# Sample value pages in TensorE: one page at a time with VectorE taking six of sixteen, against four pages at a time in four column strips

## What is computed

```python
def diff_attn(q, k, v, q_pos, k_pos, lam):
    s = jnp.einsum('bqhcd,bkhcd->bhcqk', q, k).astype(jnp.float32) * (DK ** -0.5)
    ...
    p = jax.nn.softmax(s, axis=-1)
    a = p[:, :, 0] - lam * p[:, :, 1]
    return jnp.einsum('bhqk,bkhd->bqhd', a.astype(v.dtype), v)

def mem_attn(q, mk, mv):
    ...
    return jnp.einsum('bhqm,bmhd->bqhd', p.astype(mv.dtype), mv)

k_past = cache_k[l][page_table].reshape(DB, -1, N_HEADS, 2, DK)
v_past = cache_v[l][page_table].reshape(DB, -1, N_HEADS, DV)
```

## Time and profile before

| what | value |
|---|---|
| median of 3 runs | 3238.03 us (3236.7 to 3238.45) |
| profiled execution, first to last instruction | 3223.0 us |
| around the span, up to the median | 15.0 us |
| the profiled execution's own time, taken as the median | 3238.0 us |
| TensorE busy (matmuls) | 2664.7 us, 83% |
| VectorE busy | 1416.9 us, 44% |
| GpSimd busy | 956.0 us, 30% |
| ScalarE busy | 351.2 us, 11% |
| moved by DMA | 921.73 MB, 286 GB/s |

### The profile page before, as it was taken

How to read it: one execution, slowest core, us unless ns; L and a number is a source line. 1 busy time by engine, 2 the same in 40 slices (tenths; PEclk the granted TensorE clock), 3 DMA queues, 4 the chain that set the end, 5 groups by cost and what they waited for, 6 DMA issues and landing times.

```text
span 3223.0 us, 31001 instructions
## 1 busy us (share of the span) xinstructions
PE 2664.7 (83%) x9169; PEld 1617.1 (50%) x9169; DVE 1416.9 (44%) x2212; ACT 351.2 (11%) x796; POOL 956.0 (30%) x961
## 2 busy tenths in 40 slices
PE   6899999785899999999999367776677777777778
PEld 5687888673433358888877222222222322222232
DVE  1456569533233321200026865555644444444431
ACT  3111000124200000000021000001000000011010
POOL 1256661100122210000000354444444444444432
PEclk9899999896899999999999789999999999999999
DMA  5599996740588763544434499999899999999997
GB/s 165 193 316 333 323 351 223 256 147 0 183 270 270 268 197 127 161 156 130 130 105 130 180 402 392 397 378 374 362 422 421 422 421 421 422 422 422 422 422 303
DMA packets 306118, 921.73 MB, mean 286 GB/s; under 512 B 15738, under 2 KB 196050, under 8 KB 236244
## 3 DMA queue, kind: packets, MB, share of 16 engines
q0 software_dynamic: 123488, 731.93, 57.2%
q1 hardware_dynamic: 182548, 188.92, 18.1%
HBM read 914.19 MB, written 6.63 MB: 286 GB/s over the span
## 4 chain that ended last, share of the span: by engine, by line
PE 56%; DMA 31%; DVE 6%; issue 4%; ACT 1%; POOL 1%; POOLq 0%; ACTq 0%; DVEq 0%; SPq 0%
DMA sb_hT<-in_peer_v_dram,sb_ring 26%; PE ps L531 19%; PE ps L608 10%; PE ps L814 7%; PE ps L618 5%; PE ps L719 5%; PE ps L598 3%; DMA sb_wring<-in_peer_u_dram,sb_ring 2%; DVE sb_S L1605 1%; PE ps L835 1%; POOL sb_wring L450 1%; PE ps L728 1%; PE ps L687 1%; DMA sb_bregion<-in_w_conv_out_dram 1%; PE ps L517 1%
## 5 line engine op out<-in xcount | busy, mean ns | idle before, releaser
L1605 DVE CUSTOM_DVE_ANT_0 sb_S<-sb_wring,sb_rows 128x2048 f32<-128x2048 f32 x256 | 586.9, 2292 | 542.2 <-DMA sb_wring<-in_peer_u_dram,sb_ring 531.9
L814 PE MATMUL ps<-sb_bregion,sb_ring 128*128 128x512 f32 x1024 | 490.0, 625 | 245.9 <-DMA sb_bregion<-in_peer_v_dram,sb_ring 243.8
L814 PE MATMUL ps<-sb_hT,sb_ring 128*128 128x512 f32 x1024 | 472.3, 605 | 160.9 <-DMA sb_hT<-in_peer_v_dram,sb_ring 159.9
L531 PE MATMUL ps<-sb_hT,sb_wring 128*128 128x264 f32 x2304 | 528.9, 391 | 4.6 <-ACTq L906 2.0
L531 PEld LDWEIGHTS ps<-sb_hT,sb_wring 128*128 128x128 f32 x2304 | 440.1, 192 | 85.3 <-issue 9.0
L814 PEld LDWEIGHTS ps<-sb_bregion,sb_ring 128*128 128x128 f32 x1024 | 192.7, 197 | 542.2 <-issue 241.7
L814 PEld LDWEIGHTS ps<-sb_hT,sb_ring 128*128 128x128 f32 x1024 | 185.6, 191 | 447.4 <-issue 266.0
L608 PE MATMUL ps<-sb_hT,sb_wring 128*128 128x264 f32 x1536 | 372.6, 394 | 20.6 <-DMA sb_bregion<-in_w_conv_out_dram 20.6
L450 POOL DMA_INDIRECT sb_wring<-in_peer_u_dram,sb_ring x264 | 319.8, 1211 | 214.2 <-DVEq L1062 84.9
L608 PEld LDWEIGHTS ps<-sb_hT,sb_wring 128*128 128x128 f32 x1536 | 286.5, 191 | 122.9 <-issue 77.4
L450 POOL DMA_INDIRECT sb_bregion<-in_peer_v_dram,sb_ring x132 | 154.3, 1169 | 253.2 <-PE ps L814 222.0
(11 more groups left out here) (327 smaller groups left out, 1949.6 us busy)
## 6 DMA issues: line engine op xcount, KB each, us to landing
sb_wring<-in_w_in_dram SPq DMA_DIRECT2D x52, 2048.0 KB, 11.5
sb_rows<-in_cache_v_dram POOLq DMA_DIRECT2D x128, 512.0 KB, 4.8
sb_ring<-in_cache_k_dram POOLq DMA_DIRECT2D x64, 512.0 KB, 6.3
sb_mkv<-in_cache_k_dram POOLq DMA_DIRECT2D x64, 512.0 KB, 6.3
sb_wring<-in_w_mem_kv_dram SPq DMA_DIRECT2D x8, 2048.0 KB, 9.1
sb_wring<-in_w_o_dram SPq DMA_DIRECT2D x8, 2048.0 KB, 8.0
sb_wring<-in_w_peer_q_dram SPq DMA_DIRECT2D x8, 2048.0 KB, 8.3
sb_ring<-in_cache_mem_k_dram POOLq DMA_DIRECT2D x16, 512.0 KB, 6.9
```

Of the source, the lines that this page charges most:

```text
L531: last = mm(ps[:, (2 * r + c) % 4, 0:NT], wring[:, r, k, c * P:(c + 1) * P], rhs[:, k, :], start=(k == 0), stop=(k == KC - 1))
L814: last = mm(ps[:, bank + q, :], diag[:, j % 4, :], e_slots[j % 4][:, q * 512:(q + 1) * 512], start=False, stop=False, skip_group_check=True)
L1605: st(V.tensor_tensor_reduce(out=work, in0=u_slots[slot], in1=h2, scale=1.0, scalar=0.0, op0=ALU.mult, op1=ALU.add, accum_out=out))
```

## The change

TensorE takes all 16 pages. `values` is called after steps 2, 7, 12, 17 and 22 of a chunk and takes four blocks at a time (the last time two). Block n uses the 32 columns of the array, and the 32 partitions of PSUM, that begin at 32 x (n modulo 4). Its weights are 32 columns of `zst` from its own first on, so the columns after its own heads belong to other pages. Blocks of the same strip add up in PSUM. It waits for all blocks of the group first, then goes over them once for each half of the page, so that four neighbouring matmuls lie in four strips. Each block's second matmul gives its buffer back. One ring has six buffers, in the space of the two rings before, and GpSimd issues the 18 loads of a token in order. `mask_sums` works on 64 (memory) and 128 (pages) partitions instead of 4 and 8, with `head_rows`, a 128 x 8 pattern that is 1 where a partition's number modulo 32 is the head's; three small additions make it once. It waits for the pages by `vpage_used`. `columns` of the memory blocks comes after step 8 instead of 5. VectorE's weighing is gone.

```diff
-        VR, DR = 4, 2
+        VR = 6
-        DP = 6
-        PV = 2 + PAGES - DP
-        weighed = work[:, 0:DC]
-        own_heads = [sq_mkv[0:n, o:o + DC] for n, o in ((MH, 2 * DC), (HEADS, 3 * DC))]
+        VB = 2 + PAGES
+        QUAD = 32
+        own_heads = [sq_mkv[0:n, o:o + DC] for n, o in ((2 * QUAD, 2 * DC), (P, 3 * DC))]
+        head_rows = stat[:, 48:48 + HEADS]
...
             with pool.Fori(0, TS) as b:
-                for k in range(DP):
-                    for n in (2 * k, 2 * k + 1, PV + k):
-                        if n < PV:
-                            pool.wait_ge(s["vpage_used"], b * PV + (n + 1))
-                            r = n % VR
-                        else:
-                            pool.wait_ge(s["dpage_used"], b * DP + (k + 1))
-                            r = VR + k % DR
-                        ...
-                        pool.dma_start(v_slots[r], src).then_inc(v_landed[r], 16)
+                for n in range(VB):
+                    pool.wait_ge(s["vpage_used"], b * VB + (n + 1))
+                    ...
+                    pool.dma_start(v_slots[n % VR], src).then_inc(v_landed[n % VR], 16)
...
-            def values(i, k, n):
-                if n < PV:
-                    pe.wait_ge(v_landed[n % VR], i * (4 * (PV // VR) * 16) + 16 * (PV // VR * k + n // VR + 1))
-                    block = v_slots[n % VR]
-                else:
-                    pe.wait_ge(s["weighed_ready"], i * 4 + (k + 1))
-                    block = weighed
-                ...
-                for q in range(2):
-                    last = mm(ps[0:w.shape[1], bank + q, :], w, block[:, q * 512:(q + 1) * 512], start=first, stop=final)
-                last.then_inc(s["vpage_used" if n < PV else "weighed_used"], 1)
+            def values(i, k, n0):
+                if n0 == 0:
+                    pe.wait_ge(s["sums_masked"], i * 8 + (2 * k + 1))
+                blocks = range(n0, min(n0 + 4, VB))
+                for n in blocks:
+                    pe.wait_ge(v_landed[n % VR], i * (4 * (VB // VR) * 16) + 16 * (VB // VR * k + n // VR + 1))
+                for q in range(2):
+                    for n in blocks:
+                        g = n % 4
+                        if n < 2:
+                            bank, w0, first, final = 6, PAGES * HEADS + n * MH, True, True
+                        else:
+                            bank, w0, first, final = 4, (n - 2) * HEADS, n < 6, n >= VB - 4
+                        last = mm(ps[g * QUAD:(g + 1) * QUAD, bank + q, :], zst[:, k % 2, w0:w0 + QUAD],
+                                  v_slots[n % VR][:, q * 512:(q + 1) * 512], start=first, stop=final)
+                        if q == 1:
+                            last.then_inc(s["vpage_used"], 1)
...
-                            if step % 5 in (0, 2, 4) and todo:
-                                values(i, k, todo.pop(0))
-                            if step == 5:
+                            if step % 5 == 2:
+                                values(i, k, 4 * (step // 5))
+                            if step == 8:
                                 columns(i, k, 0)
...
+            st(TT(head_rows[:, :], ident[:, 0:HEADS], ident[:, QUAD:QUAD + HEADS], ALU.add))
+            st(TT(head_rows[:, :], head_rows[:, :], ident[:, 2 * QUAD:2 * QUAD + HEADS], ALU.add))
+            st(TT(head_rows[:, :], head_rows[:, :], ident[:, 3 * QUAD:3 * QUAD + HEADS], ALU.add))
...
-                n = (MH, HEADS)[kind]
-                if kind == 0:
-                    dve.wait_ge(s["vpage_used"], i * (4 * PV) + (PV * k + 2 + VR))
-                else:
-                    dve.wait_ge(s["weighed_used"], i * 4 + (k + 1))
+                n, heads = own_heads[kind].shape[0], (MH, HEADS)[kind]
+                dve.wait_ge(s["vpage_used"], i * (4 * VB) + (VB * k + (2, VB)[kind] + VR))
...
-            def weigh_page(i, k, j):
-                ...
-            with st.loop((16 - PART) // 4, 4 * (3 + DP * HEADS)) as i:
+            with st.loop((16 - PART) // 4, 4 * 3) as i:
                 for q in range(4):
-                    dve.wait_ge(s["weights_staged"], i * 4 + (q + 1))
-                    for j in range(DP):
-                        weigh_page(i, q, j)
-                        if j == 1:
-                            mask_sums(i, q, 0)
-                    signal("weighed_ready")
+                    mask_sums(i, q, 0)
                     mask_sums(i, q, 1)
```

More of the change, by code:

```diff
@@ L206, in build @@
             diag_ready v_used yo_full y_ready y_stored hb_used zero_ready dve_done act_done pool_done
-            n2_in lam_pre lam_exp x1_rows n2_ss sums_free weights_staged dpage_used weighed_ready
-            weighed_used sums_masked columns_done sub_taken gather_turn loop_turn""".split()
+            n2_in lam_pre lam_exp x1_rows n2_ss sums_free weights_staged
+            sums_masked columns_done sub_taken gather_turn loop_turn""".split()
         s = {n: sem(n) for n in names}
@@ L212, in build @@
         k_landed = [sem(f"k_landed{i}") for i in range(8)]
-        v_landed = [sem(f"v_landed{i}") for i in range(VR + DR)]
+        v_landed = [sem(f"v_landed{i}") for i in range(VR)]
         qb_landed = [sem(f"qb_landed{i}") for i in range(2)]
@@ L414, in _ @@
             with pool.Fori(0, TS) as b:
-                for k in range(DP):
-                    for n in (2 * k, 2 * k + 1, PV + k):
-                        if n < PV:
-                            pool.wait_ge(s["vpage_used"], b * PV + (n + 1))
-                            r = n % VR
-                        else:
-                            pool.wait_ge(s["dpage_used"], b * DP + (k + 1))
-                            r = VR + k % DR
-                        if n < 2:
-                            src = cmem_v[ds(b * NM + n * P, P), :]
-                        else:
-                            page = pool.value_load(pt[0:1, ds(b * PAGES + (n - 2), 1)], min_val=0, max_val=POOL_PAGES - 1)
-                            src = cache_v[ds(page * PAGE, PAGE), :]
-                        pool.dma_start(v_slots[r], src).then_inc(v_landed[r], 16)
-            pool.wait_ge(s["vpage_used"], TS * PV + VR)
-            pool.wait_ge(s["dpage_used"], TS * DP + DR)
+                for n in range(VB):
+                    pool.wait_ge(s["vpage_used"], b * VB + (n + 1))
+                    if n < 2:
+                        src = cmem_v[ds(b * NM + n * P, P), :]
+                    else:
+                        page = pool.value_load(pt[0:1, ds(b * PAGES + (n - 2), 1)], min_val=0, max_val=POOL_PAGES - 1)
+                        src = cache_v[ds(page * PAGE, PAGE), :]
+                    pool.dma_start(v_slots[n % VR], src).then_inc(v_landed[n % VR], 16)
+            pool.wait_ge(s["vpage_used"], TS * VB + VR)
             pool.dma_start(x_rows[:, 0:2, :], A["x_prompt"][0].rearrange("(t p) d -> p t d", p=P)).then_inc(s["x_again"], 16)
@@ L1413, in mask_sums @@
             def mask_sums(i, k, kind):
-                n = (MH, HEADS)[kind]
-                if kind == 0:
-                    dve.wait_ge(s["vpage_used"], i * (4 * PV) + (PV * k + 2 + VR))
-                else:
-                    dve.wait_ge(s["weighed_used"], i * 4 + (k + 1))
+                n, heads = own_heads[kind].shape[0], (MH, HEADS)[kind]
+                dve.wait_ge(s["vpage_used"], i * (4 * VB) + (VB * k + (2, VB)[kind] + VR))
                 dve.wait_ge(s["columns_done"], i * 8 + (2 * k + kind + 3))
-                as_heads = lambda ap: ap.rearrange("p (h c) -> p h c", h=n)
+                as_heads = lambda ap: ap.rearrange("p (h c) -> p h c", h=heads)
                 st(TT(as_heads(own_heads[kind]), as_heads(ps[0:n, 6 - 2 * kind:8 - 2 * kind, :].rearrange("p a b -> p (a b)")),
-                      ident[0:n, 0:n].unsqueeze(2).broadcast_to([n, n, DC // n]), ALU.mult))
+                      head_rows[0:n, 0:heads].unsqueeze(2).broadcast_to([n, heads, DC // heads]), ALU.mult))
                 signal("sums_masked")
-            def weigh_page(i, k, j):
[L1430 to L1441, removed]
-            with st.loop((16 - PART) // 4, 4 * (3 + DP * HEADS)) as i:
-                for q in range(4):
-                    dve.wait_ge(s["weights_staged"], i * 4 + (q + 1))
-                    for j in range(DP):
-                        weigh_page(i, q, j)
-                        if j == 1:
-                            mask_sums(i, q, 0)
-                    signal("weighed_ready")
+            with st.loop((16 - PART) // 4, 4 * 3) as i:
+                for q in range(4):
+                    mask_sums(i, q, 0)
                     mask_sums(i, q, 1)
```

3 lines of the change are left out of this document (removed).

## The result

| | before | after |
|---|---|---|
| median | 3238.24 us (4 runs, 3236.7 to 3239.45) | 3277.44 us (4 runs, 3270.49 to 3281.2) |
| ratio | | 1.0116, 95% interval 1.0096 to 1.0136 |
| profiled execution, span | 3223.0 us | 3276.0 us |
| sample stage, first gate step to last columns | 333.6 us | 385.6 us |
| behind the stage: to the experts / experts | 693.4 / 1355.5 us | 695.8 / 1353.0 us |

A forecast was written before the change was run, and what follows sets the result against it. TensorE bounds the kernel before; its whole saving turns into waiting for pages (stage 333 us, as before), and half clock adds 50: 383 against 333. Added to 3238.03, that makes 3288 us, range 3225 to 3355.

The forecast's parts named there:

- The saving on TensorE: Sample stage: four strips overlap fully, 2.0 us a visit, five visits instead of 13; 121 us saved if pages always there.
- (d): Rival, chance 0.20: strips take turns, 52.2 us a chunk; 101 us more, 3339, with some half clock 3370.
- (e): Rival, chance 0.12: two strips run at a time, visit 3.7 us, stage +54 us and a little clock, 3305.
- VectorE's work worth nothing: Sample stage: taking the weighing off VectorE gains nothing by itself, as it is done before TensorE asks.
- The ring: Sample stage: reissued pages put 7.5 us between a visit's end and the next start; stage 333 us, as long as before.
- The clock: Sample stage: bursts after page waits begin at 1.2 GHz, three visits a chunk 1.7 us longer; 50 us in all.
- rival (b): Chance 0.10: strips overlap but the clock holds in the sample stage; time 3238, within 0.2%.
- The sum: Sample stage 333 + 50 = 383 us against 333, +50; whole time 3288.
- 15.0 us lie around it: Whole kernel before: 15.0 us added to the profiled span of 3223.0 to reach the median of 3238.03.
- The faster rival (c): Chance 0.13: pages land at 3.7 us, second of a pair under about 4, clock mostly holds; time 3203.
- Price of taking turns: Sample stage, if the strips take turns: 11.4 us from visit to visit, 101 us more than before.

The follow-up runs named there:

- pairs6: The changed kernel with visits of two blocks in two strips instead of four, ring of six kept: 3201.44 us, ratio 0.9896 to before.
- ring8: The changed kernel with eight page buffers instead of six, groups of four kept: 3174.88 us, ratio 0.9812 to before.
- serial: The changed kernel with all blocks sent to the first strip of 32 columns instead of four strips: 3357.55 us, ratio 1.0389 to before.

## Why the prediction was right, and where not

- **The saving on TensorE.** Full overlap was taken from two row halves in the earlier trace rows; in the trace after, a full visit takes 1.85 us from its first matmul to the next gate matmul at full clock, and 2.0 was put in with the change-over. Right. Rivals (d) and (e) fall. The whole saving with pages always there was put at 121 us; without loads it is 107 of stage, and the 12 us lost at the ends of the chunks are most of the difference.
- **VectorE's work worth nothing.** VectorE's work in the stage fell to 23 us and the stage got longer. Whether taking the work away from VectorE gains anything was not tried by itself.
- **The ring.** 7.5 us from end to start of a visit were put in and 7.3 are measured in the link shown. With the 12 us for the weight loads spread over the 24 links, 8.0 were put in, and 7.9 is the mean. The mechanism held under two edits from either side, fewer blocks held (pairs6) and more buffers (ring8). Landings had a median of 5.1, not 4.8.
- **The clock.** 24 visits at half clock and 50 us were forecast. 25 of 40 start at half clock, filling the waits gave back 35 us of stage, and rival (b), clock holds, falls. The near match of the counts is luck in part: "each burst that follows a page wait begins at 1.2 GHz" holds for 18 of the 23 visits behind a page wait, and 7 visits start slow behind none. The sum held better. The visits take 2.85 us in the mean, 113.9 us together, against 74.1 at full clock: 40 us more, where 3 x 1.7 x 8 = 41 were put in. The end of a chunk was mis-sized: from the end of the fourth visit to the next chunk's first 9.1 us and 1.1 for the clock were put in, and the mean is 11.5. Without the half clock in both places, and with the links as long as they are, after's 385.6 us would be some 330. That is an estimate: 385.6 less the 40 of the visits and less 7 x 2.3, the chunk ends above the 9.2 us that they take at full clock. It is as forecast for full clock (333) and no longer than before. By this reckoning the half clock is the whole loss of the stage, and what the ring costs at full clock is what the strips save, as forecast. The added matmuls alone show 35 of the 52 us.
- **The sum.** The stage was forecast at 383 us and measured at 385.6. The time was forecast at 3288 and is 3277.44. The term that was off is "15.0 us lie around it". After, the profiled execution took 3277.62 us with a span of 3276.0, so only 1.6 us lie around a span. By the same 1.6 us (1.64 in serial and 1.68 in ring8 as well) the execution before with the span of 3223.0 us was itself one of some 3225 us, 13 under the median; single runs of before lay between 3221.12 and 3245.51 us in the later sessions. 3225 + 52 = 3277. Trace against trace the difference is the stage's 52; median against median it is 39, since before's trace is of an execution faster than all four that were timed. Where the median execution before spends its 13 us more is open, since no trace of one was taken; in the traces here the part ahead of the first gate chunk ends anywhere from 617 to 627 us.
- **The faster rival (c).** It needed second pages landing under 4 us. In the link shown it was 4.66 us from the second issue to the visit's start. Falls.
- **Price of taking turns.** Forecast 101 us over before, measured 126 by the ratio of 1.0389, as visit to visit is 12.6 us in the mean (1052.81 to 1065.20 in that trace, for example), not 11.4; 9 of the 40 visits start at half clock too.

## To carry to other kernels

When an engine is made to take its inputs in larger groups, count what the group holds until its end against the ring: with a group of four in a ring of six, each group waits for release, issue and landing of two pages, 7 to 8 us here, while the DMA engines are busy for only 0.65 of the stage. A saving on TensorE that turns into idle gaps was paid a second time here, as the clock came down on the burst that lies between landing and release. The same change with eight or nine buffers is a gain here: size the ring at two groups before making the groups.

## What the hardware showed that was not expected

- Four fp32 matmuls with 32 columns each, over all 128 partitions, run at the same time almost without loss: 16 records of 512 columns in 1.85 us, in one strip 6.96 us, 3.8 times, or 0.94 a strip. The Trainium skill (TensorE: Matmul & The Clock Gate, Measured speedup vs the span model) has 2.38 times for three column tiles, which is 0.79 a tile. The traces here give more for four, and the measurement decides; three were not tried.
- The clock also fell where TensorE counts as busy throughout. In the run without loads, 931.5 to 934.9 us count 3.40 of 3.40 us busy, and the granted clock is 0.62 in the mean: ahead lay a wait of 0.94 us and 16 records of one column each, still at full clock up to 932.3 us, and the clock fell to 1.2 GHz behind them (0.50 from 933 to 935 us).
- Matmuls that nobody reads made the kernel 27 us faster by the medians (24 by the ratios): with them 30 of the 40 visits start at 2.4 GHz, without them 15.
